# Gathering an expert's first features transposed, and reloading its first places in parts

## The chip, the cores and the metric

The kernel runs on one core of one Trainium2 chip. The metric is the device time of one execution, in microseconds (us). Before the change the median of three runs is 1217.37 us (1217.15 to 1218.14).

## What is computed

256 tokens with 2048 features pass through one layer: a gMLP mixer with its residual, then a mixture of 16 experts, two of which are chosen for each token, then an RMS norm. Of the reference, the part that matters here:

```python
def expert_block(args):
    xblk, e = args
    hid = jax.nn.silu(xblk @ w_gate[e]) * (xblk @ w_up[e])
    return hid @ w_down[e]
```

`w_gate` and `w_up` are 2048 x 1024 for each expert and `w_down` is 1024 x 2048, all float32: 25.2 MB for an expert and 403 MB for the sixteen. Each must be read once.

## The kernel before

**Mixer and router.** The mixer runs until about 290 us of the profile; its products leave the residual stream in `x` (two blocks of 128 tokens on the partitions, 2048 features along them). TensorE, ScalarE and VectorE then work out the router: scores, the two experts of each token, and the rank of each token within its expert. From the ranks VectorE builds `pick` (128 tokens by 64 slots, for each block), a selection matrix that carries the norm's scale.

**Experts as items.** An item is one expert with up to 64 of its tokens. Its weights come in twelve *units* of 2 MB (128 partitions by 4096 numbers, which are 4 rows of 1024 for gate and up): gate 0 and 1, up 0 and 1 (these four use the first half of the features, `xg_a`), gate 2 and 3, up 2 and 3 (second half, `xg_b`), then four units of `w_down`. `gate_or_up` (L1223) multiplies one unit: for each of four rows `s`, two products with 64 columns of features as the left (stationary) operand and 512 columns of weights moving. Each product in float32 is two passes in the profile. After its last product a unit increments `step_done`. So item 0 ends with step 12, and step 16 is the fourth unit of item 1.

**Features.** `gather` (L1178) multiplies `pick` (left) by `x` (moving), which gives rows of tokens in `bank[6]` and `bank[7]`; `x_row` takes a bank (ScalarE for the first half, VectorE for the second), `transpose_rows` (L1188) turns it with four transposes, and `take_half` (L879, VectorE) scales it into `xg_a` or `xg_b`. For item 0 the first half is on the way of everything that follows; for later items this is done during the item before.

**Places and loads.** There are ten places for units in `blocks` and `late` and an eleventh in `acc`. All loads are issued by SyncE on one queue, in the order written, each after a wait. The first eleven units of expert 0 fill all places. Then a load can only be issued when TensorE has used up a place: `HOMES[0]` is reloaded in three parts (row 0, row 1, rows 2 and 3; waits on `first_row_used` and on step 1), and then one unit follows on each step: expert 1's unit 1 on step 2, expert 0's last unit on step 3, expert 1's unit `n` on step `n + 2` up to unit 8, and units 9, 10 and 11 on steps 12, 13 and 14. From expert 2 on, pairs of units are loaded with one DMA of 4 MB (`load_quad`, L381), the first of them on step 16. Counted in units, 13 are loaded between the first reload and this pair.

**VectorE around it** works down a fixed program: the router's chain, `take_half(0, 0)`, then some twenty small instructions that make the table of items, a register load of the item count, `take_second_row(0)` (L933), `take_half(0, 1)`. TensorE, ScalarE and SyncE read the item count into a register as well.

Of the kernel before, what the change touches and what calls it, by code (L numbers as in the profile page):

```python
# [15 lines left out]
def hybrid_trunk_kernel(nc, x_in, norm_mix_g, norm_ffn_g, final_g, a_w_in, a_v_gain, a_w_s, a_b_s,  # L16
# [38 lines left out]
    with ExitStack() as ctx:  # L55
# [127 lines left out]
        row_loaded = [sem(f"row_loaded{s}") for s in range(2)]  # L183
        first_row_used = sem("first_row_used")
# [80 lines left out]
        FIRST_LOAD = [(single_loaded[h], 16) for h in FIRST_AT[0:SLOTS + 1]] + [(single_loaded[2], 32)]  # L265
        SECOND_AT = [SINGLES.index((unit // 2 % PAIRS, unit % 2)) for unit in range(ITEM_DOUBLES)]
        SECOND_LOAD = [(single_loaded[h], 48 if h == 2 or unit >= SLOTS else 32) for unit, h in enumerate(SECOND_AT)]
# [56 lines left out]
        def _(sp):  # L324
# [58 lines left out]
            for q in range(SLOTS + 1):  # L383
                if q == 1:

                    sp.wait_ge(mixed, HEADS)
                elif q in (3, 4, 6, 7):

                    sp.wait_ge(tile_split, KD * (PIECES - 1) + 4 * (q - 2 if q < 5 else q - 3))
                elif q == 5:  # L390

                    sp.wait_ge(tile_used, KD * (PIECES - 1) + KD // 2)
                elif q == 8:

                    sp.wait_ge(tile_used, KD * PIECES)
                elif q == 9:

                    sp.wait_ge(quarters_done, 1)
                elif q == SLOTS:

                    sp.wait_ge(sq_v_done, NB)
                load_half(0, UNIT_AT[q], HOMES[q], single_loaded[q])

            for s in range(2):

                sp.wait_ge(first_row_used, s + 1)
                sp.dma_start(HOMES[0][:, s * F:(s + 1) * F], source(1, 0)[:, s * F:(s + 1) * F]).then_inc(row_loaded[s], 16)
            sp.wait_ge(step_done, 1)
            sp.dma_start(HOMES[0][:, 2 * F:4 * F], source(1, 0)[:, 2 * F:4 * F]).then_inc(single_loaded[0], 16)

            sp.wait_ge(step_done, 2)
            load_half(1, 1, HOMES[1], single_loaded[1])
            sp.wait_ge(step_done, 3)
            load_half(0, SLOTS + 1, HOMES[2], single_loaded[2])
            for unit in range(2, SLOTS - 1):

                sp.wait_ge(step_done, unit + 2)
                load_half(1, unit, HOMES[SECOND_AT[unit]], SECOND_LOAD[unit][0])
# [94 lines left out]
        def _(act):  # L513
# [81 lines left out]
            act.wait_ge(gathered, 1)  # L595
            nc.scalar.copy(x_row, bank[6][:, :]).then_inc(row_a_ready, 1)
# [64 lines left out]
        def _(dve):  # L661
# [220 lines left out]

            count = bank[3][:, 0:E]
# [12 lines left out]
            take_half(0, 0)  # L896
# [69 lines left out]

            take_second_row(0)
# [16 lines left out]
        def _(pe):  # L984
# [189 lines left out]
            def gather(jj, halves=range(2)):  # L1174

                for b in range(NB):
                    for h in halves:
                        last = T.matmul(bank[6 + jj][h * TOK:(h + 1) * TOK, :], pick[:, b, :],  # L1178
                                        columns_of(x[:, b, jj * PIECE:(jj + 1) * PIECE], h),
                                        start=(b == 0), stop=(b == NB - 1))  # L1180
                if 1 in halves:
                    last.then_inc(gathered, 1)

            def transpose_rows(n, jj):

                pe.wait_ge((row_a_ready, row_b_ready)[jj], n + 1)
                for s in range(4):
                    last = T.transpose(bank[6 + jj][:, s * P:(s + 1) * P], every(4, x_row, s), ident[:, :])  # L1188
                last.then_inc(row_transposed, 1)
# [17 lines left out]
            gather(0)  # L1207
            gather(1, halves=(0,))
            transpose_rows(0, 0)
            gather(1, halves=(1,))  # L1210
# [3 lines left out]
            def item(i, first=False, last=False):  # L1214

                def gate_or_up(unit):
                    weights = slot_of(i, unit, last)
                    pe.wait_ge(*load_of(i, unit, last))
                    for s in range(4):
                        if isinstance(i, int) and i == 1 and unit == 0 and s < 2:  # L1220
                            pe.wait_ge(row_loaded[s], 16)
                        for c in range(2):
                            ins = T.matmul(bank[unit // 2 % 2][c * TOK:(c + 1) * TOK, :], xg(unit // 4 * 8 + unit % 2 * 4 + s),  # L1223
                                            weights[:, s * F + c * BANK:s * F + (c + 1) * BANK],
                                            start=(unit in (0, 2) and s == 0), stop=(unit in (GU - 3, GU - 1) and s == 3))
                        if first and unit == 0 and s < 2:
                            ins.then_inc(first_row_used, 1)
                    ins.then_inc(step_done, 1)

                pe.wait_ge(xg_ready, i * 2 + 1)  # L1230
                gate_or_up(0)
                if not first:
# [3 lines left out]
                for unit in range(1, 4):  # L1236
                    if not first:
                        scatter((i - 1) * 8, (2 * unit - 2, 2 * unit - 1))
                    gate_or_up(unit)
                    if first and unit == 1:  # L1240
                        transpose_rows(0, 1)
                if not first:
                    scatter((i - 1) * 8, (6, 7))
                if first:
                    pe.wait_ge(xg_ready, 2)
# [102 lines left out]
```

## Time and profile before

| what | value |
|---|---|
| median of three runs | 1217.37 us |
| the profiled execution | 1218.12 us |
| its span | 1216.1 us |
| TensorE busy | 1151.1 us, 95% of the span |
| VectorE busy | 371.8 us, 31% |
| ScalarE busy | 109.7 us, 9% |
| DMA, mean over the span | 379 GB/s, 460.70 MB |
| TensorE's granted clock | 0.990 of full speed |

The time of an execution is the span from the first to the last instruction and 2.0 us around it. The page's row of the DMA rate in 40 slices shows 150 to 360 GB/s in the mixer, 408, 330 and 367 in the three slices from 243 to 334 us, and 429 to 433 in nearly all from there to the end. A busy TensorE is no sign of a bound by itself: its passes are counted while they are in flight.

### The profile page before, as it was taken

To read this page: it belongs to the slowest core of one execution; us is meant where nothing else is said; L and a number is where in the kernel's file an instruction comes from. 1 tells how busy PE (TensorE), PEld (TensorE's weight loads), DVE (VectorE), ACT (ScalarE), POOL (GpSimd) and SP (SyncE) were. 2 spreads that over 40 slices of the span, in tenths; PEclk is the share of its full clock that TensorE was granted. 3 is DMA by queue.
4 is the path that set the end of the run, shared out by engine and by line. 5 is a ranking of instruction groups with operands and counts; after the bars stand their busy time and mean duration, and the time that the engine had idled before them with its cause. 6 is when DMAs were issued, how large, how long until landed. Compare 5 with 4: busy or idle time off the path is not lost.

```text
span 1216.1 us, 12008 instructions
## 1 busy us (share of the span) xinstructions
PE 1151.1 (95%) x5197; PEld 524.8 (43%) x5197; DVE 371.8 (31%) x560; ACT 109.7 (9%) x186; POOL 7.5 (1%) x24
## 2 busy tenths in 40 slices
PE   9999999999999999999989898989899898989986
PEld 7888877887333333333323232323232233323321
DVE  6867787776222111112111111111111111111112
ACT  1303002012010000000000000000000000000003
POOL 0200000000000000000000000000000000000000
PEclk9999999999999999999999999999999999999999
DMA  9856544598999999999999999999999999999995
GB/s 357 331 194 193 193 173 151 203 408 330 367 430 433 429 431 431 431 433 431 431 431 432 431 432 432 431 432 431 429 432 433 429 431 431 431 432 429 426 417 208
DMA packets 36303, 460.70 MB, mean 379 GB/s; under 512 B 4360, under 2 KB 5920, under 8 KB 21792
## 3 DMA queue, kind: packets, MB, share of 16 engines
q1 hardware_dynamic: 36208, 459.97, 90.9%
q8 instruction: 41, 0.67, 0.2%
q14 instruction: 6, 0.05, 0.0%
q10 hardware_dynamic: 48, 0.01, 0.0%
HBM read 457.87 MB, written 2.10 MB: 378 GB/s over the span
## 4 chain that ended last, share of the span: by engine, by line
PE 64%; DMA 32%; SPq 1%; DVE 1%; ACT 1%; issue 0%; ACTq 0%; DVEq 0%
PE bank L1223 25%; DMA blocks<-in_moe_w_gate 17%; DMA blocks<-in_moe_w_up 10%; PE bank L1286 8%; PE kept L1030 4%; PE kept L1032 4%; PE kept L1031 4%; PE bank L1030 4%; PE bank L1032 3%; PE bank L1031 3%; PE kept L1197 3%; DMA blocks<-in_moe_w_down 3%; PE kept L1178 3%; DMA late<-in_moe_w_gate 2%; PE kept L1188 1%; SPq L457 1%
## 5 line engine op out<-in xcount | busy, mean ns | idle before, releaser
L924 DVE TENSOR_TENSOR acc<-acc,kept 128x512 f32<-128x512 f32 x120 | 77.1, 684 | 455.5 <-PE kept L1197 455.5
L1223 PE MATMUL bank<-blocks,xg_a 128*64 128x512 f32 x832 | 196.4, 614 | 19.7 <-DMA blocks<-in_moe_w_gate 17.8
L1286 PE MATMUL bank<-blocks,sil 128*64 128x512 f32 x800 | 178.1, 599 | 12.2 <-DMA blocks<-in_moe_w_down 12.2
L1223 PE MATMUL bank<-blocks,xg_b 128*64 128x512 f32 x752 | 166.5, 594 | 3.2 <-DMA blocks<-in_moe_w_gate 1.6
L1223 PEld LDWEIGHTS bank<-blocks,xg_a 128*64 128x64 f32 x832 | 59.7, 140 | 149.9 <-issue 140.8
L690 DVE TENSOR_TENSOR w_lo<-blocks,w_hi 128x1024 fp32r<-128x1024 f32 x96 | 117.7, 1226 | 3.2
L1286 PEld LDWEIGHTS bank<-blocks,sil 128*64 128x64 f32 x800 | 56.1, 138 | 124.8 <-issue 104.1
L1223 PEld LDWEIGHTS bank<-blocks,xg_b 128*64 128x64 f32 x752 | 52.4, 137 | 114.6 <-issue 99.1
L951 DVE TENSOR_TENSOR sil<-sil,bank 128x512 f32<-128x512 f32 x16 | 11.0, 688 | 253.4 <-PE bank L1223 253.4
L683 DVE CAST w_hi<-blocks 128x1024 fp32r<-128x1024 f32 x96 | 67.2, 700 | 64.6 <-PE kept L1032 30.4
L1197 PE MATMUL kept<-y,back 64*128 64x512 f32 x240 | 67.7, 641 | 0.0
L1223 PE MATMUL bank<-late,xg_b 128*64 128x512 f32 x272 | 60.4, 595 | 2.8 <-DMA late<-in_moe_w_gate 2.2
L1178 PE MATMUL kept<-x,pick 128*64 128x512 f32 x256 | 62.9, 599 | 0.0
L1223 PE MATMUL bank<-late,xg_a 128*64 128x512 f32 x192 | 45.3, 614 | 5.6 <-DMA late<-in_moe_w_gate 5.4
L602 ACT ACTIVATE sil<-bank 128x512 f32<-128x512 f32 x16 | 9.6, 597 | 429.2 <-PE bank L1223 429.2
L1197 PEld LDWEIGHTS kept<-y,back 64*128 64x128 f32 x240 | 18.1, 184 | 48.9 <-issue 48.9
L1030 PE MATMUL kept<-w_hi,act_second 128*128 128x512 f32 x96 | 38.3, 398 | 0.0
L1030 PE MATMUL kept<-w_hi,act_first 128*128 128x512 f32 x96 | 38.2, 397 | 0.0
L1223 PEld LDWEIGHTS bank<-late,xg_b 128*64 128x64 f32 x272 | 18.9, 137 | 43.5 <-issue 35.7
L1030 PE MATMUL bank<-w_hi,act_second 128*128 128x512 f32 x96 | 37.6, 391 | 0.0
L1032 PE MATMUL kept<-w_hi,act_second 128*128 128x512 f32 x96 | 37.4, 390 | 0.0
L1032 PE MATMUL kept<-w_hi,act_first 128*128 128x512 f32 x96 | 37.4, 390 | 0.0
(205 smaller groups left out, 941.5 us busy)
## 6 DMA issues: line engine op xcount, KB each, us to landing
blocks<-in_moe_w_down SPq DMA_DIRECT2D x21, 4096.0 KB, 39.9
blocks<-in_moe_w_gate SPq DMA_DIRECT2D x20, 4096.0 KB, 40.1
blocks<-in_moe_w_up SPq DMA_DIRECT2D x20, 4096.0 KB, 40.2
blocks<-in_a_w_in SPq DMA_DIRECT2D x31, 1024.0 KB, 6.1
late<-in_moe_w_gate SPq DMA_DIRECT2D x6, 4096.0 KB, 34.2
late<-in_moe_w_up SPq DMA_DIRECT2D x6, 4096.0 KB, 40.6
blocks<-in_moe_w_down SPq DMA_DIRECT2D x11, 2048.0 KB, 14.6
blocks<-in_moe_w_gate SPq DMA_DIRECT2D x9, 2048.0 KB, 14.4
```

The source lines that it names most:

```text
L457: sp.dma_start(home, src).then_inc(loaded, 16)
L683: V.tensor_copy(w_hi[:, k % 2, :], raw).then_inc(hi_split, 1)
L690: V.tensor_tensor(w_lo[:, k % 2, :], raw, w_hi[:, k % 2, :].bitcast(f32), ALU.subtract)\
L924: V.tensor_tensor(acc[:, b, cols], acc[:, b, cols], bank[5 + j % 3][:, :], ALU.add)\
L1030: T.matmul(dst, hi, wh, start=(k == 0), stop=False)
L1031: T.matmul(dst, hi, wl, start=False, stop=False)
L1032: last = T.matmul(dst, lo, wh, start=False, stop=(k == KD - 1))
L1178: last = T.matmul(bank[6 + jj][h * TOK:(h + 1) * TOK, :], pick[:, b, :], columns_of(x[:, b, jj * PIECE:(jj + 1) * PIECE], h), start=(b == ...
L1188: last = T.transpose(bank[6 + jj][:, s * P:(s + 1) * P], every(4, x_row, s), ident[:, :])
L1197: T.matmul(bank[5 + j % 3][:, :], back[h * TOK:(h + 1) * TOK, b * P:(b + 1) * P], y[h * TOK:(h + 1) * TOK, jj, :], start=True, stop=True). ...
L1223: ins = T.matmul(bank[unit // 2 % 2][c * TOK:(c + 1) * TOK, :], xg(unit // 4 * 8 + unit % 2 * 4 + s), weights[:, s * F + c * BANK:s * F + ...
L1286: ins = T.matmul(bank[2 + c // 2][at:at + TOK, :], hidden, weights[:, s * D + c * BANK:s * D + (c + 1) * BANK], start=(j == 0 and s == 0), ...
```

## The change

Three things change, for item 0 and the reloads that follow it alone.

1. `gather_features` takes the place of `gather`, the copy, and `transpose_rows` for the first half of the features: `x` is the left operand (128 tokens by 128 features, every eighth) and `pick` the moving one (64 columns), so features come out on the partitions at once. It is two products for each of eight groups of features: four groups for `bank[5]` and one for `bank[6]` ahead of the first unit, three more behind it. VectorE's `take_features` scales each bank (128 by 256) into `xg_a`; the second of them stands behind the table of items. The gather of the second half (`gather(1)`) moves behind the third unit, and its transposes behind the fourth.
2. `FIRST_ORDER` exchanges the second and the third unit of expert 0: up 0 comes second, which needs the same four groups of features as gate 0.
3. The first six places are reloaded in parts (`PARTS`): places 0, 1 and 3 in rows 0, 1 and 2 to 3; places 2, 4 and 5 in two halves. The semaphore `part_used` counts the parts. It makes 15 DMAs where there were 8.

TensorE's program from the router's end to item 0's fifth unit, before (`kept` is a PSUM bank; `xg_a`, `xg_b` are the features):

```order
L1178 MATMUL kept<-x,pick 64x512 x6
L1188 MATMUL kept<-ident,y 128x128 x4
L1178 MATMUL kept<-x,pick 64x512 x2
L1212 TENSOR_LOAD before_last
L1212 ISA x2
L1223 MATMUL bank<-blocks,xg_a 64x512 x16
L1188 MATMUL kept<-ident,y 128x128 x4
L1223 MATMUL bank<-blocks,xg_a 64x512 x16
L1223 MATMUL bank<-blocks,xg_b 64x512 x16
```

And with the change:

```order
L1195 MATMUL kept<-pick,x 128x64 x10
L1237 TENSOR_LOAD before_last
L1237 ISA x2
L1247 MATMUL bank<-blocks,xg_a 64x512 x8
L1195 MATMUL kept<-pick,x 128x64 x6
L1247 MATMUL bank<-blocks,xg_a 64x512 x16
L1203 MATMUL kept<-x,pick 64x512 x4
L1247 MATMUL bank<-blocks,xg_a 64x512 x8
L1215 MATMUL kept<-ident,y 128x128 x4
L1247 MATMUL bank<-blocks,xg_b 64x512 x16
```

Eight gathering products and four transposes stood ahead of the first unit, ten small products stand there now; six small ones, four gathering ones and the transposes have moved between the units, and the transposes stand directly ahead of the fifth.

SyncE's queue behind the first eleven units, before:

```order
L407 DMA blocks<-in_moe_w_gate 128x1024 [waits first_row_used] x2
L409 DMA blocks<-in_moe_w_gate 128x2048 [waits step_done]
L373 DMA blocks<-in_moe_w_gate 128x4096 [waits step_done]
L373 DMA blocks<-in_moe_w_down 128x4096 [waits step_done]
L373 DMA blocks<-in_moe_w_up 128x4096 [waits step_done] x2
```

And with the change:

```order
L425 DMA blocks<-in_moe_w_gate 128x1024 [waits part_used] x2
L425 DMA blocks<-in_moe_w_gate 128x2048 [waits step_done]
L425 DMA blocks<-in_moe_w_gate 128x1024 [waits part_used] x2
L425 DMA blocks<-in_moe_w_gate 128x2048 [waits step_done]
L425 DMA blocks<-in_moe_w_down 128x2048 [waits part_used]
L425 DMA blocks<-in_moe_w_down 128x2048 [waits step_done]
L425 DMA blocks<-in_moe_w_up 128x1024 [waits part_used] x2
```

The same bytes go in the same order; a load that waited for its whole unit now follows row by row.

The diff, cut to its core:

```diff
         loop_half_loaded = sem("loop_half_loaded")
-        row_loaded = [sem(f"row_loaded{s}") for s in range(2)]
-        first_row_used = sem("first_row_used")
+        part_used = sem("part_used")
+        first_features_ready = sem("first_features_ready")
         ident_ready = sem("ident_ready")
...
         FIRST_HOME = [HOMES[h] for h in FIRST_AT]
-        FIRST_LOAD = [(single_loaded[h], 16) for h in FIRST_AT[0:SLOTS + 1]] + [(single_loaded[2], 32)]
+        FIRST_ORDER = [0, 2, 1] + list(range(3, ITEM_DOUBLES))
+        PARTS = {0: (1, 2, 4), 1: (1, 2, 4), 2: (2, 4), 3: (1, 2, 4), 4: (2, 4), 5: (2, 4)}
+        WHOLE = (4,)
         SECOND_AT = [SINGLES.index((unit // 2 % PAIRS, unit % 2)) for unit in range(ITEM_DOUBLES)]
-        SECOND_LOAD = [(single_loaded[h], 48 if h == 2 or unit >= SLOTS else 32) for unit, h in enumerate(SECOND_AT)]
+        RELOADS = [(1, 0), (1, 1), (0, SLOTS + 1)] + [(1, unit) for unit in range(2, SLOTS - 1)]
+
+        def reloaded(place_no):
+
+            return 16 + 16 * len(PARTS.get(place_no, WHOLE))
+
+        FIRST_LOAD = [(single_loaded[h], 16) for h in FIRST_AT[0:SLOTS + 1]] + [(single_loaded[2], reloaded(2))]
+        SECOND_LOAD = [(single_loaded[SECOND_AT[unit]], reloaded(unit if unit < 2 else unit + 1)) for unit in range(SLOTS - 1)]
+        SECOND_LOAD += [(single_loaded[SECOND_AT[SLOTS - 1 + n]], reloaded((2, 0, 1)[n]) + 16) for n in range(3)]
...
                     sp.wait_ge(sq_v_done, NB)
-                load_half(0, UNIT_AT[q], HOMES[q], single_loaded[q])
-
-            for s in range(2):
-
-                sp.wait_ge(first_row_used, s + 1)
-                sp.dma_start(HOMES[0][:, s * F:(s + 1) * F], source(1, 0)[:, s * F:(s + 1) * F]).then_inc(row_loaded[s], 16)
-            sp.wait_ge(step_done, 1)
-            sp.dma_start(HOMES[0][:, 2 * F:4 * F], source(1, 0)[:, 2 * F:4 * F]).then_inc(single_loaded[0], 16)
-
-            sp.wait_ge(step_done, 2)
-            load_half(1, 1, HOMES[1], single_loaded[1])
-            sp.wait_ge(step_done, 3)
-            load_half(0, SLOTS + 1, HOMES[2], single_loaded[2])
-            for unit in range(2, SLOTS - 1):
-
-                sp.wait_ge(step_done, unit + 2)
-                load_half(1, unit, HOMES[SECOND_AT[unit]], SECOND_LOAD[unit][0])
+                load_half(0, FIRST_ORDER[UNIT_AT[q]], HOMES[q], single_loaded[q])
+
+            parts_used = 0
+            for n, (expert, unit) in enumerate(RELOADS):
+
+                done = 0
+                for upto_row in PARTS.get(n, WHOLE):
+                    if upto_row < 4:
+                        parts_used += 1
+                        sp.wait_ge(part_used, parts_used)
+                    else:
+                        sp.wait_ge(step_done, n + 1)
+                    at = unit % 2 * 2 * HALF
+                    sp.dma_start(FIRST_HOME[n][:, done * PIECE:upto_row * PIECE],
+                                 source(expert, unit // 2)[:, at + done * PIECE:at + upto_row * PIECE])\
+                      .then_inc(single_loaded[FIRST_AT[n]], 16)
+                    done = upto_row
             for unit in range(SLOTS - 1, ITEM_DOUBLES):
...
                                      bias=red[:, b, 1:2], accum_out=red[:, b, 2:3]).then_inc(exp_done, 1)
-            act.wait_ge(gathered, 1)
-            nc.scalar.copy(x_row, bank[6][:, :]).then_inc(row_a_ready, 1)
             act.wait_ge(count_ready, 1)
...
+            def take_features(h):
+
+                V.tensor_tensor(xg_a[:, 4 * h:4 * h + 4, :], bank[5 + h][:, 0:4 * TOK].rearrange("p (s t) -> p s t", s=4),
+                                row_gain[:, 4 * h:4 * h + 4].unsqueeze(2).to_broadcast([P, 4, TOK]), ALU.mult)\
+                 .then_inc((first_features_ready, xg_ready)[h], 1)
+
...
                                  ALU.mult))
-            take_half(0, 0)
+            dve.wait_ge(gathered, 1)
+            take_features(0)
             link(V.tensor_tensor(start[:, 0, :], upto[:, 0, :], extra[:, 0, :], ALU.subtract))
...
+            dve.wait_ge(row_transposed, 1)
+            take_features(1)
             take_second_row(0)
...
-            def gather(jj, halves=range(2)):
+            def gather_features(h, rows):
+
+                for s in rows:
+                    for b in range(NB):
+                        last = T.matmul(bank[5 + h][:, s * TOK:(s + 1) * TOK], every(8, x[:, b, 0:PIECE], 4 * h + s),
+                                        pick[:, b, :], start=(b == 0), stop=(b == NB - 1))
+                return last
+
+            def gather(jj):
                 for b in range(NB):
-                    for h in halves:
+                    for h in range(2):
                         last = T.matmul(bank[6 + jj][h * TOK:(h + 1) * TOK, :], pick[:, b, :],
...
                                         start=(b == 0), stop=(b == NB - 1))
-                if 1 in halves:
-                    last.then_inc(gathered, 1)
+                last.then_inc(gathered, 1)
...
-                pe.wait_ge((row_a_ready, row_b_ready)[jj], n + 1)
+                if jj == 0:
+                    pe.wait_ge(row_a_ready, n)
+                else:
+                    pe.wait_ge(row_b_ready, n + 1)
                 for s in range(4):
...
             pe.wait_ge(pick_ready, 1)
-            gather(0)
-            gather(1, halves=(0,))
-            transpose_rows(0, 0)
-            gather(1, halves=(1,))
+            gather_features(0, range(4)).then_inc(gathered, 1)
+            gather_features(1, (0,))
             pe.wait_ge(count_ready, 1)
...
-                def gate_or_up(unit):
-                    weights = slot_of(i, unit, last)
-                    pe.wait_ge(*load_of(i, unit, last))
+                def gate_or_up(n):
+                    weights = slot_of(i, n, last)
+                    unit = FIRST_ORDER[n] if first else n
+                    pe.wait_ge(*load_of(i, n, last))
                     for s in range(4):
-                        if isinstance(i, int) and i == 1 and unit == 0 and s < 2:
-                            pe.wait_ge(row_loaded[s], 16)
                         for c in range(2):
...
                                             start=(unit in (0, 2) and s == 0), stop=(unit in (GU - 3, GU - 1) and s == 3))
-                        if first and unit == 0 and s < 2:
-                            ins.then_inc(first_row_used, 1)
+                        if first and s < 3 and s + 1 in PARTS.get(n, WHOLE):
+                            ins.then_inc(part_used, 1)
                     ins.then_inc(step_done, 1)
-                pe.wait_ge(xg_ready, i * 2 + 1)
+                if first:
+                    pe.wait_ge(first_features_ready, 1)
+                else:
+                    pe.wait_ge(xg_ready, i * 2 + 1)
                 gate_or_up(0)
-                if not first:
+                if first:
+                    gather_features(1, range(1, 4)).then_inc(row_transposed, 1)
+                else:
                     pe.wait_ge(y_ready, i)
...
                         scatter((i - 1) * 8, (2 * unit - 2, 2 * unit - 1))
+                    if first and unit == 2:
+                        pe.wait_ge(xg_ready, 1)
                     gate_or_up(unit)
-                    if first and unit == 1:
-                        transpose_rows(0, 1)
+                    if first and unit == 2:
+                        gather(1)
                 if not first:
...
                 if first:
+                    transpose_rows(0, 1)
                     pe.wait_ge(xg_ready, 2)
...
                 gate_or_up(5)

```

## Rows read from the trace of the kernel before

**Rows 1.** Stretches of the program, from the windows view; columns: engines, clock, DMA share, GB/s.

```profile
305.00:321.00 16.00, 16.00 (x76) 6.33 (x74) 6.47 (x22) 0.00 (x0) 0.00 (x0) 1.00 0.88 313
321.00:1150.00 829.00, 782.04 (x3512) 258.40 (x3509) 127.17 (x232) 50.16 (x92) 0.00 (x0) 0.99 1.00 431
```

**Rows 2.** The chain that ended last, at its end: start, us, what.

```profile
1154.90 39.13 DMA blocks<-in_moe_w_down
...
1194.08 3.65 PE bank L1298 x16
```

**Rows 3.** The same chain around expert 0 and the start of expert 1.

```profile
287.77 2.00 PE kept L1016 x16
289.77 1.91 PE bank L1151 x32
...
298.63 3.58 PE kept L1178 x12
...
302.89 1.43 PE kept L1178 x3
304.32 0.07 PE bank L1223
...
311.62 0.68 PE kept L1188 x4
312.30 13.88 PE bank L1223 x64
...
335.28 1.72 PE kept L1178 x8
...
357.65 3.58 PE bank L1223 x16
...
370.52 1.06 PE kept L1197 x4
```

**Rows 4.** The timeline of VectorE between the router and expert 0's second features.

```profile
299.98 0.19 DVE L894 TENSOR_TENSOR weight_of<-wsel,red 128x32 f32<-128x32 f32 x1
303.00 0.69 DVE L879 TENSOR_TENSOR xg_a<-kept,row_gain 128x512 f32<-128x512 f32 x1 [2.82 <-PE kept L1188]
303.61 0.17 DVE L897 TENSOR_TENSOR start<-upto,extra 128x16 f32<-128x16 f32 x1
...
309.47 0.18 DVE L917 CAST item_expert<-ids_f 128x24 int32<-128x24 f32 x1
310.69 0.69 DVE L933 COPY y<-kept 128x512 f32<-128x512 f32 x1 [1.04 <-issue]
```

**Rows 5.** Issues of loads on SyncE's queue, from its timeline.

```profile
305.64 1.19 SPq L407 DMA_DIRECT2D blocks<-in_moe_w_gate  x2
...
315.92 0.33 SPq L373 DMA_DIRECT2D blocks<-in_moe_w_down  x1
...
370.56 0.33 SPq L381 DMA_DIRECT2D blocks<-in_moe_w_gate  x1
```

**Rows 6.** Loads issued at 284.04, 287.80, 361.28, 370.56; the last column is us to landing.

```profile
blocks<-in_moe_w_up SPq DMA_DIRECT2D x1, 2048.0 KB, 7.3
...
late<-in_moe_w_down SPq DMA_DIRECT2D x1, 2048.0 KB, 9.6
...
blocks<-in_moe_w_down SPq DMA_DIRECT2D x1, 2048.0 KB, 14.3
...
blocks<-in_moe_w_gate SPq DMA_DIRECT2D x1, 4096.0 KB, 14.8
```

**Rows 7.** The DMA engines when their queue had run empty, in windows of 1 us.

```profile
283.00:284.00 1.00, 1.00 (x5) 0.56 (x3) 1.00 (x1) 0.00 (x0) 0.00 (x0) 1.00 0.00 0
284.00:285.00 1.00, 0.99 (x5) 0.80 (x5) 0.01 (x1) 0.00 (x0) 0.00 (x0) 1.00 0.23 49
285.00:286.00 1.00, 1.00 (x6) 0.81 (x5) 0.24 (x1) 0.00 (x0) 0.00 (x0) 1.00 0.89 213
```

**Rows 8.** TensorE's first wait for a load of expert weights, in the waits of 580 to 640.

```profile
PE bank L1223 <- DMA blocks<-in_moe_w_gate: 2.9, 2, 2.7
```

## The prediction, made before the changed kernel was run

> **What bounds the kernel now.** I read the windows first, then the chain that ended last, then SyncE's issues with their landings. From 321 to 1150 us the DMA engines are busy without a break and move 431 GB/s, while TensorE's clock stays at 0.99; only from 305 to 321 us do they fall to 313 GB/s [rows 1]. The chain ends in a load that lands at 1194.03, followed by expert work and the output [rows 2]. TensorE meets its first wait for a weight load between 580 and 640 us [rows 8]. So the end of the kernel is the end of a stream of loads that is full from 321 us on, and a change near 300 us is worth what it moves the *stream*, not what it moves TensorE. What the stream lost near 305 is 16 us x (1 - 313/431) = 4.4 us [rows 1]. It was lost because all places were full and the first reload waits for TensorE: the first unit starts at 304.32 [rows 3], its first rows are given back at 305.64 [rows 5]. 4.4 us is the most the change can earn there.
>
> **Term 1, the first unit starts earlier.** TensorE begins the gather at 298.63 [rows 3]. The new gather ahead of the first unit is eight products, 16 passes, each with its own load of a 128 x 128 piece of `x`. No row has just this. The nearest is L1016, also a strided 128 x 128 piece of `x` as left operand: 16 passes in 2.00 us, 0.125 us each, with 128 columns moving where here there are 64 [rows 3]. I take 0.125. From below, the router's passes cost 1.91/32 = 0.060; from above, the four scatter passes cost 1.06/4 = 0.265, and nearer, four row transposes 0.68/4 = 0.17 [rows 3]. So the bank is full at 300.6, seen by VectorE 0.1 later, at 300.7. VectorE's chain is through by then (L894 ends at 300.17 [rows 4]). `take_features` has 256 elements: between 0.19 us for 32 and 0.69 us for 512 [rows 4] that is 0.19 + 0.50 x 224/480 = 0.42. The first unit starts at about 301.2 instead of 304.32, **3.1 us earlier**. The two passes for group 4 need 0.5 us and lie beside VectorE's work. The register load on TensorE may delay this: on VectorE the whole step took 1.04 us [rows 4], from the end of L917. On TensorE it can start when `before_last` is there, some instructions before L894 (299.98 [rows 4]), and I cost it at nothing if it runs while the passes are still in the queue; without that cover, 0.3 to 0.9 us.
>
> **Term 2, what has moved between the units.** Behind the first unit stand six products, 12 passes x 0.125 = 1.5. A unit costs 3.58 behind other work and 3.43 behind a unit ((13.88 - 3.58)/3), a gather of four products 1.72, and the transposes 0.68 [rows 3]. The second bank of features costs TensorE nothing: the table of items ends 6.04 us after the first scaling's successor starts (303.61 to 309.65 [rows 4]), so at about 307.1, plus 1.04 and 0.42 is 308.6, and the third unit wants it at 301.2 + 3.43 + 1.5 + 3.58 = 309.7. If that cover goes, the third unit is late by the rest. At the fourth unit's end the second half of the features is late next: the transposes now stand directly ahead of the fifth unit, and `take_half` between them is bare: 0.11 to hand over (transposes done at 302.89 [rows 3], scaling from 303.00 [rows 4]), 0.69 [rows 4] and an estimated 0.06 back, 0.86. The fifth unit thus starts at 301.2 + 3.43 + 1.5 + 7.01 + 1.72 + 3.58 + 0.68 + 0.86 = 319.98. Before it started at 312.30 + 13.88/2 = 319.24 [rows 3]. **TensorE is 0.75 us later** from there on, although it began 3.1 us earlier: the transposed gather moves 28 passes of 0.125 (3.5 us) in the place of one gather and one turn, and the turn that was between units 2 and 3 has its scaling in the open. From the fifth unit to step 16 TensorE's chain has no wait for a load, so the 0.75 us stays.
>
> **Term 3, the reloads.** A unit's reload goes out 3.62 us after the unit starts (312.30 to 315.92 [rows 3, 5]), a row's 0.86 us per row after it. With an empty queue data flow at the full rate from about 1.4 us after the issue: 284.04, and 431 - 49 plus 431 - 213 missing in two windows [rows 7]. The stream, 4.87 us per unit of 2.1 MB, needs unit *u* issued by 305.0 + 4.87u - 1.4. The parts go out at about 302.2, 303.1 and 304.8 (u = 0, needed by 303.6), 307.2 (u = 1, by 308.5), 311.6 (u = 2, by 313.3), 315.9 (u = 3, by 318.2), 321.9 (u = 4, by 323.1). So the whole 4.4 us are won back by 321. The parts are needed for it: a whole unit at 309.8, for u = 1, would come 1.3 too late.
>
> **Term 4, the cap.** What counts is whether TensorE can keep giving back places to a stream that is 4.4 us earlier. The tight point is the first pair, 4 MB, on step 16: issued at 370.56 [rows 5], directly at the end of a unit on a chain of TensorE alone [rows 3]. It has 13 units ahead of it. Before, it landed 14.8 us after its issue [rows 6]. With an empty queue it would land after 7.3 for the first 2 MB [rows 6], and 6.1 for the second (287.80 + 9.6 less 284.04 + 7.3 [rows 6]), 13.4 together. **The slack is 1.4 us**: however early the stream is, the pair cannot land more than 1.4 us earlier than it did, plus or minus what its issue moves. By bytes alone the slack is smaller: 5.0 MB moved by 321 [rows 1], 22.2 MB more of the 13 units at 431 GB/s end at 372.6, against 370.56 + 1.4, so 0.7. With 4.87 instead of 6.1 for the second half it is 14.8 - 12.2 = 2.6. I take 1.4, as landings are what TensorE waits for, and keep 0.7 and 2.6. After the pair the issues at later steps have more room, and the DMA engines hold the kernel to its end.
>
> **Sum.** Won: 4.4 us at 321, capped at 1.4 by step 16, less the 0.75 by which step 16 is later: 0.65 us. Against the profiled execution: 1218.12 - 0.65 = 1217.5; the median shown is 0.75 below that execution, so 1217.37 - 0.65 = **1216.7 us**.
>
> By the Trainium skill (TensorE: Matmul & The Clock Gate, "LDWEIGHTS (loading the stationary operand)") a weight load takes its columns divided by 1.2 in ns, 107 ns for 128 columns, however few columns move behind it. By it 28 passes would be 0.5 us shorter than by L1016's 0.125, and the sum 1216.2; I stay with the row.
>
> **The rivals.**
> *The cap does not bind.* If step 16 comes earlier than I think, or the pair lands with the rest of the stream, what is won at 321 stays, less a gap at the reload on step 12 of some 1.4: 4.4 - 1.4 = 3.0, **1214.4**. For it: the DMA engines were busy without a gap at 372. Against it: the issue at 370.56 and its landing 14.8 later, little over the 13.4 of an empty queue.
> *TensorE's new passes are dear* (the other side). If strided loads of `x` do not hide beside so short a moving part, a pass costs the 0.265 of the scatter rows: 28 x 0.14 = 3.9 us, step 16 is 4.65 us later, less 1.4: 3.25 us slower, **1220.6**. It decides from a delay of 3.8 us, a pass of 0.235. For it: the moving part has only 64 columns to hide a load behind. Against it: L1016 loads the same kind of piece at 0.125.
> *Small parts slow the stream.* 15 loads instead of 8 for 12.6 MB. It becomes slower than before by 2.4 us if the six units lose 4.4 + 2.4 = 6.8 of their 29.2 us, below 350 GB/s. A price between 313 GB/s (with its gaps) and 431 [rows 1]: in the middle, 372, the six units lose 4.6, which takes up the 4.4 and 0.2 more, **1217.6**; at 313 they lose 11, which is the far end, 1224. Against it: parts behind others in a full queue left no dip that I can find. The Trainium skill (DMA: Bandwidth & Descriptors, "Measured (HBM→SBUF, 128 partitions, SWDGE, issued from GpSimd)") wants 1 MiB or more in a load and gives 341 GB/s for 1 MB; by it, an estimate, the six units would take 7.7 us more and the kernel 3.3 us more, 1220.7. That figure is for loads one at a time from another engine.
> *The change does not do what it says:* if the register load holds TensorE until after 301.9, step 16 moves by 1.5 and nothing is won: 1217.4.
>
> **How the numbers follow.** About 0.2% (2.4 us) is what a measurement of this kernel tells from no change, so faster means below 1214.9, slower above 1219.8. My forecast, with the register load's case in it: 0.72. Its own ends: passes at 0.060 save 0.5 ahead of the first unit (VectorE's chain holds it at 300.17) and 0.8 behind it, so step 16 is 0.5 early, and with the slack of 2.6 it is 1214.3; passes at 0.17 and the slack of 0.7 give 1217.37 + 2.0 - 0.7 = 1218.7. Cap not binding: 0.15. Dear passes: 0.07. Small parts: 0.06. The range takes most of the forecast and of the first rival: 1214.4 to 1218.7. Faster: 0.15 and 0.03 of my own tail, 0.18. Slower: 0.07 and 0.02. Same: 0.73.
>
> **What would show it.** Right: first unit at 301.2, TensorE's new passes at 0.12 to 0.13, fifth unit at 320.0, no dip of the DMA rate at 305 to 321, a new dip of some 3 to 4 us just ahead of the pair's issue at 371.3, and its landing 13.4 after that. Wrong: a rate of 431 through 366 to 373 (no cap), passes of 0.2 or more, a wait of the third unit for VectorE, or a dip that stays at 305 to 321.

## The result, and the profile after

The changed kernel takes 1222.79 us (median of five runs, 1222.40 to 1224.14), beside 1217.36 us for the kernel before in the same comparison (five runs). The ratio is 1.0052, with a 95% interval from 1.0041 to 1.0063. The change is slower, by **5.4 us** between the medians; the interval of the ratio spans 5.0 to 7.7 us. The forecast was 1216.7, with a range to 1218.7. Its profiled execution took 1224.01 us, with a span of 1221.9, against 1218.12 and 1216.1 before.

The windows view of the changed kernel, for the stretches of [rows 1] and three between them (start:end, us, then PE, PEld, DVE, ACT and POOL busy, granted clock, DMA share, GB/s):

```profile
305.00:321.00 16.00, 16.00 (x72) 7.13 (x70) 4.45 (x15) 0.00 (x0) 0.00 (x0) 0.96 0.85 275
321.00:366.00 45.00, 43.84 (x206) 15.38 (x204) 6.55 (x15) 6.70 (x8) 0.00 (x0) 1.00 1.00 410
366.00:375.00 9.00, 9.00 (x41) 2.58 (x39) 2.57 (x4) 0.00 (x0) 0.00 (x0) 1.00 1.01 431
375.00:420.00 45.00, 44.70 (x210) 15.25 (x206) 6.19 (x12) 3.11 (x6) 0.00 (x0) 1.00 0.99 418
420.00:1150.00 730.00, 683.21 (x3058) 225.26 (x3054) 112.25 (x204) 39.62 (x77) 0.00 (x0) 0.99 1.00 431
```

The stream of loads should have had no dip at 305 to 321. It has a deeper one, 275 GB/s for 313 before, and it loses again in the next 100 us; from 420 on it is the 431 GB/s of before. The bound is the same, the stream has lost more. The chain of waits says why. Its part that answers to [rows 3] (start, us, what):

```profile
298.31 4.95 PE kept L1195 x20
303.27 5.12 PE bank L1247 x16
308.39 3.00 PE kept L1195 x12
311.39 7.02 PE bank L1247 x32
318.40 1.72 PE kept L1203 x8
320.12 3.43 PE bank L1247 x16
323.56 0.69 PE kept L1215 x4
324.25 0.02 issue
324.27 0.70 DVE xg_b L887
324.97 0.04 issue
325.02 7.09 PE bank L1247 x32
```

Two things are not as forecast. The new passes (L1195) take 4.95/20 = 0.248 and 3.00/12 = 0.250 us, for 0.125. And the first unit, 16 passes that cost 3.43 to 3.58 us everywhere in [rows 3], takes 5.12. The new line by shape (duration min/median/max in ns):

```profile
L1195 PEld LDWEIGHTS kept<-pick,x x32: 312/334/336, 298.2 to 310.9; 128*128 128x128 f32 x32
L1195 PE MATMUL kept<-pick,x x32: 401/401/452, 298.2 to 311.0; 128*128 128x64 f32 x32
```

And TensorE's granted clock around the start of the first unit, in windows of the same view:

```profile
302.50:303.00 0.50, 0.50 (x4) 0.50 (x3) 0.47 (x3) 0.00 (x0) 0.00 (x0) 0.93 0.54 229
303.00:306.00 3.00, 3.00 (x9) 1.03 (x11) 2.69 (x10) 0.00 (x0) 0.00 (x0) 0.50 0.63 268
306.00:306.50 0.50, 0.50 (x4) 0.05 (x2) 0.43 (x3) 0.00 (x0) 0.00 (x0) 0.65 1.06 139
```

From about 302.9 to 306.3 it is 0.50, the lower of its two levels (1.2 for 2.4 GHz). It was 1.00 in the same windows before, and what stands ahead of the drop is TensorE busy without a gap, with the new passes. SyncE's issues answer to [rows 5]:

```profile
305.21 0.33 SPq L425 DMA_DIRECT2D blocks<-in_moe_w_gate  x1
...
376.49 0.33 SPq L391 DMA_DIRECT2D blocks<-in_moe_w_gate  x1
```

The first row of the first place goes out at 305.21 (before 305.64, forecast 302.2), the pair on step 16 at 376.49, 5.9 us later than the 370.56 before. VectorE's part was as costed: `take_features` takes 0.42 us, and the table of items ends at 308.75, long before the third unit.

### The profile page after: what moved, and what is told of

Its sections match the earlier page's. It is cut to its first block, busy times and chain, and to the rows that moved or that the text cites. A ratio compares the mean times of both kernels' runs of the same rounds, so it can differ in the third digit from the quotient of the medians.

```text
span 1221.9 us, 12056 instructions
## 1 busy us (share of the span) xinstructions
PE 1155.7 (95%) x5217; PEld 530.2 (43%) x5217; DVE 371.5 (30%) x561; ACT 109.2 (9%) x185; POOL 7.5 (1%) x24
## 4 chain that ended last, share of the span: by engine, by line
PE 62%; DMA 34%; SPq 1%; DVE 1%; ACT 1%; issue 0%; ACTq 0%; DVEq 0%
PE bank L1247 24%; DMA blocks<-in_moe_w_gate 20%; PE bank L1318 7%; DMA blocks<-in_moe_w_up 7%; DMA blocks<-in_moe_w_down 6%; PE kept L1047 4%; PE kept L1049 4%; PE kept L1048 4%; PE bank L1047 3%; PE bank L1049 3%; PE bank L1048 3%; PE kept L1224 3%; PE kept L1203 2%; DMA late<-in_moe_w_gate 2%; SPq L467 1%; PE kept L1215 1%
## 5 line engine op out<-in xcount | busy, mean ns | idle before, releaser
L1247 PE MATMUL bank<-blocks,xg_a 128*64 128x512 f32 x832 | 199.0, 622 | 20.8 <-DMA blocks<-in_moe_w_gate 19.9
L1203 PE MATMUL kept<-x,pick 128*64 128x512 f32 x248 | 59.2, 598 | 0.0
L1048 PE MATMUL bank<-w_lo,act_second 128*128 128x512 f32 x96 | 37.4, 389 | 0.0
```

Of the source, the lines that this page charges most:

```text
L1048: T.matmul(dst, hi, wl, start=False, stop=False)
```

## The experiments

The rival "TensorE's new passes are dear" had come, with something on top. **Theory A** says that the piece of `x` with every eighth feature is slow to load as a left operand, that this alone makes the pass 0.25 us and lets the clock drop, and that all that is lost follows from TensorE's delay. **Theory B** says that the short moving part (64 columns) has nothing to hide a load behind, so any such pass costs this. **Theory C** puts a share of the loss on the small reloads. Before each verdict stands what was expected; the kernel before was timed beside each (1216.77, 1217.05 and 1216.76 us in three comparisons, the first for e1 to e4, the second for e5, e7, e10 and e11, the third for the rest).

### e1: the same products, with contiguous pieces of x

```diff
-every(8, x[:, b, 0:PIECE], 4 * h + s)
+x[:, b, (4 * h + s) * P:(4 * h + s + 1) * P]
```

> The changed kernel, but the left operand of the transposed gather takes 128 consecutive features instead of every eighth; the features then stand in another order than the weights want, and nothing else differs. Theory A, the step of the left operand sets the price: a pass falls from 0.25 us to 0.12 us (12 passes behind the first unit in 1.5 us instead of 3.0), the clock stays at full speed, step 16 is issued 5 us earlier than in the changed kernel and the time is 1216.7 to 1217.5 us. Theory B, a short moving part cannot hide any load of 128 columns: 0.25 us a pass, the clock drops as before, 1222.8 us.

Measured: 1216.58 us, ratio 1.0000 [0.9991, 1.0009]. Its chain of waits, first units and fifth:

```profile
298.76 1.95 PE kept L1195 x16
...
301.28 3.65 PE bank L1247 x16
304.94 1.48 PE kept L1195 x12
...
320.04 7.09 PE bank L1247 x32
```

Its windows:

```profile
305.00:321.00 16.00, 15.22 (x78) 6.16 (x80) 4.70 (x15) 0.00 (x0) 0.00 (x0) 1.00 1.00 404
321.00:366.00 45.00, 44.63 (x210) 15.36 (x208) 6.19 (x12) 6.70 (x8) 0.00 (x0) 1.00 1.01 417
366.00:375.00 9.00, 9.00 (x40) 2.58 (x38) 2.57 (x4) 0.00 (x0) 0.00 (x0) 1.00 0.91 359
```

A pass costs 1.95/16 = 0.122 us, the clock stays at 1.00, the first unit starts at 301.28 and the fifth at 320.04. Nothing but the step between the features of the left operand was changed, so it carries the whole loss, and theory B falls: 64 columns behind a contiguous load are cheap. This is also the kernel that the forecast had described, with the dip at 305 nearly gone and a new one at 366 to 375. Its time, 1216.58 for 1216.7, flatters the forecast: beside the kernel before of its own comparison (1216.77) it won 0.2 us, not told from nothing, where 0.65 was forecast.

### e2: the reloads in parts alone, on the kernel before

```diff
-            for s in range(2):
-                sp.wait_ge(first_row_used, s + 1)
...
+            for n, (expert, unit) in enumerate(RELOADS):
+                for upto_row in PARTS.get(n, WHOLE):
...
```

> The kernel before with the reloads of the first six places in parts and nothing else of the change: TensorE's work is as before. Theory cap (the pair of loads on step 16 sets the stream): the dip at 305 to 321 shrinks by 2 to 3 us and comes back ahead of the pair's issue, gain 0.7 to 1.4 us, 1216.0 to 1216.7 us. Theory stream (what is won at 321 stays): 1214.4 to 1215. Theory small parts slow the stream: slower than 1217.4, rate under 400 GB/s at 321 to 345.

Measured: 1215.68 us, ratio 0.9995 [0.9986, 1.0004]; 360 GB/s at 305 to 321 for 313, 401 at 366 to 375 for 435. Not told from no change. The parts fill the first dip in part, and most of that is given back ahead of step 16. Theory C finds nothing here.

### e3: 26 passes more on TensorE between the fourth and the fifth unit of the kernel before

```diff
                 if first:
+                    keep_warm(4, 13)
                     pe.wait_ge(xg_ready, 2)
```

> The kernel before with 13 idle products of 128 columns (0.235 us each, 3.05 us) on TensorE between the fourth and fifth unit of expert 0, so that step 16 is 3.05 us late and the stream up to 321 us is as before. Theory cap with a slack of 0.7 to 1.4: slower by 1.6 to 2.4 us, 1219.0 to 1219.7. With a slack of 2.6: 1217.8. If step 16 does not set the stream: no change.

Measured: 1219.74 us, ratio 1.0023 [1.0012, 1.0034]. The chain shows the added wait for what it is:

```profile
319.54 3.10 PE kept L992 x26
322.64 7.02 PE bank L1223 x32
```

3.1 us of delay cost 2.8 us by the ratio and 3.0 by the medians. That is more than any of the three expectations (at most 2.4), so TensorE had nearly no slack in giving back places here. The stream runs at 412 GB/s in 321 to 366 and 406 in 366 to 375: it loses at several reloads, not at the pair alone.

### e4: every fourth feature in place of every eighth

Gate and up of expert 0 are loaded with four rows per partition, so that the left operand has a step of four. The result is the same.

```diff
-every(8, x[:, b, 0:PIECE], 4 * h + s)
+every(4, x[:, b, h * BANK:(h + 1) * BANK], s)
```

> The changed kernel with expert 0's weights for gate and up loaded with four rows of features to a partition instead of eight, so that the transposed gather takes every fourth feature (the same result is computed). Theory A, price by the step: 0.125 us a pass like the transposes with the same step, clock at full speed, step 16 at 371.3 us, 1216.7 to 1217.5 us. Theory B: 0.25 us a pass and 1222.8 us. A third, any step above one costs 0.25: as B here, while the contiguous one is cheap.

Measured: 1222.28 us, ratio 1.0039 [1.0025, 1.0052]. From its chain and its windows:

```profile
298.73 4.87 PE kept L1203 x20
303.60 5.87 PE bank L1256 x16
309.46 2.94 PE kept L1203 x12
```

```profile
302.00:303.50 1.50, 1.50 (x7) 1.41 (x7) 0.70 (x3) 0.00 (x0) 0.00 (x0) 0.50 0.89 371
303.50:308.00 4.50, 4.50 (x13) 1.40 (x14) 4.02 (x15) 0.00 (x0) 0.00 (x0) 0.50 0.78 278
```

The form of theory A that I had written down, by which a step of four loads at the transposes' price, is wrong: a pass is 0.245 us. The clock dropped earlier, inside the first gather at about 301.4, and stayed at 0.50 until about 308.2. Nearly half of the first twenty passes ran at 0.50, yet the twenty cost 4.87/20 = 0.244, and the twelve at full clock 2.94/12 = 0.245. The pass with this operand does not depend on TensorE's clock; the unit behind it does.

### e5: 128 columns moving behind the same strided pieces

```diff
-pick[:, b, :]
+pick[:, b:b + 1, :].to_broadcast([P, 2, TOK])
```

> The changed kernel with the moving operand of the transposed gather given twice, 128 columns instead of 64 (the second copy isn't read). Theory load-bound: a pass stays at 0.25 us, since the load of the strided left operand takes that long and the moving part hides beside it. If the clock fell because too little moved through TensorE in these passes, it now stays at full speed, the first unit takes 3.5 instead of 5.1 us and the time is 1.7 us below the changed kernel, about 3.7 us over the kernel before. If the moving part had been bare beside the load, a pass grows to 0.30 and the time rises by 1.5 us.

Measured: 1220.30 us, ratio 1.0027 [1.0018, 1.0037].

```profile
299.11 4.96 PE kept L1195 x20
304.06 3.58 PE bank L1247 x16
307.64 3.05 PE kept L1195 x12
```

```profile
303.00:306.00 3.00, 3.00 (x15) 1.64 (x16) 2.51 (x10) 0.00 (x0) 0.00 (x0) 1.00 0.84 360
```

Twice the columns cost nothing, so the pass waits for its load alone. And with them the clock stays at 1.00 and the first unit is back at 3.58 us. That parts the two costs: 3.25 us slower than before with the dear passes alone, 5.4 with the drop. By the chain the drop is 5.12 - 3.58 = 1.5 us in the profiled execution of the changed kernel.

### e7: the changed kernel with places 1 to 5 reloaded whole

```diff
-PARTS = {0: (1, 2, 4), 1: (1, 2, 4), 2: (2, 4), 3: (1, 2, 4), 4: (2, 4), 5: (2, 4)}
+PARTS = {0: (1, 2, 4)}
```

> The changed kernel with places 1 to 5 reloaded whole, as in the kernel before (place 0 stays in parts). Theory cap: step 16 sets the stream, so the parts are worth little here: the DMA rate at 305 to 321 falls by 40 GB/s or more and the time stays within 1 us of the changed kernel. Theory stream: it is 2 us or more slower than the changed kernel.

Measured: 1222.22 us, ratio 1.0040 [1.0026, 1.0054], against 1.0052 with the parts; the two intervals overlap. 236 GB/s at 305 to 321, but 420 at 321 to 366. The chain has the first unit longer than in the changed kernel:

```profile
303.13 5.97 PE bank L1247 x16
```

The clock was at 0.50 here from about 301.1 to 307.9, as long as in e4, so this trace holds 0.85 us of delay that has nothing to do with the parts. Neither e2 nor e7 shows a cost or a gain of the parts; the 0.6 us between the medians and this delay leave room for a share of some 1.4 us in the changed kernel. Theory C is not needed, but it isn't ruled out to the last microsecond.

### e10: contiguous pieces, features early, and the first pairs in halves

The three repairs that the runs above suggest, with the same result. Gate and up of expert 0 are loaded in the order that contiguous pieces need; the gather of the second half stands ahead of the third unit and its transposes behind it, so that VectorE's scaling lies under the fourth; and expert 2's four pairs are loaded in halves, the first of each one step earlier.

```diff
+gate_k = w_gate[0].rearrange("e (j s p) c -> p e j s c", p=P, s=4)
...
-every(8, x[:, b, 0:PIECE], 4 * h + s)
+x[:, b, (4 * h + s) * P:(4 * h + s + 1) * P]
...
                     gate_or_up(unit)
-                    if first and unit == 2:
+                    if first and unit == 1:
                         gather(1, first=True)
+                    if first and unit == 2:
+                        transpose_rows(0, 1)
...
+                if n in pair_half_loaded:
+                    for h in range(2):
+                        sp.wait_ge(step_done, 2 * (n - PAIRS + 1) + ITEM_DOUBLES - 1 + h)
+                        load_half(n // ITEM_QUADS + 1, n % ITEM_QUADS * 2 + h, QUADS[quad_at(n)][:, h, :],
...
```

> The changed kernel with three further edits: expert 0's gate and up weights are loaded in the layout in which consecutive features make a left operand (a pass of 0.12 us), the second half's gather stands ahead of the third unit and its turn behind it (its scaling no longer in the open, 0.8 us), and expert 2's first four pairs are loaded in halves, the first on the step before (the cap on step 16 moves). All the same result. If the cap is what held the stream back, 2 to 3.5 us faster than the kernel before, no dip at 366 to 375. If the cap isn't it, at most 1.2 us faster.

Measured: **1213.65 us**, ratio 0.9970 [0.9959, 0.9980], the fastest of all.

```profile
298.61 1.95 PE kept L1216 x16
...
301.13 3.65 PE bank L1271 x16
304.79 1.48 PE kept L1216 x12
306.27 3.58 PE bank L1271 x16
309.85 1.72 PE kept L1224 x8
311.57 3.43 PE bank L1271 x16
315.00 0.59 PE kept L1237 x4
315.59 10.45 PE bank L1271 x48
```

```profile
305.00:321.00 16.00, 16.00 (x82) 6.25 (x83) 4.56 (x14) 0.00 (x0) 0.00 (x0) 1.00 1.01 412
...
366.00:375.00 9.00, 9.00 (x42) 2.70 (x40) 2.57 (x4) 0.00 (x0) 0.00 (x0) 1.00 1.01 428
```

The rate shows no dip any more, and TensorE goes from the transposes into the fourth unit, and through three units, without waiting for VectorE.

### e11, e12 and e9: the halves with and without the rest

e11 is the kernel before with the parts of e2 and the halves of e10; e12 the kernel before with the halves alone; e9 is e10 without them (its expectation calls e10 the run before last).

```diff
+                if n in pair_half_loaded:
+                    for h in range(2):
...
```

> The kernel before with reloads in parts and expert 2's first four pairs in halves; TensorE's work and order as before. The parts alone won 1.3 us of DMA time by 366 and gave 0.5 back by 375. With the halves nothing is given back: 1.2 to 1.8 us faster than the kernel before. If the halves change nothing: as the parts alone, 0.5 to 1.1 us faster.

> The kernel before with expert 2's first four pairs loaded in halves, the first half one step earlier, and nothing else. In the kernel before the queue still held loads when step 16 came (no dip at 366 to 375), so by theory cap nothing is won alone: within 0.5 us of the kernel before. If issuing earlier helps by itself: 1 us or more faster.

> The kernel of the run before last but with expert 2's pairs loaded whole again, that is the changed kernel with consecutive features as left operand and the second half's gather ahead of the third unit; the same result. If step 16 caps the stream: the dip comes back at 366 to 375 (rate under 380 GB/s) and of the 3.4 us at least 1.5 are lost again, 1215 to 1216 us. If the halves were idle, 1213.7.

Measured: e11 1216.26 us, 0.9993 [0.9984, 1.0002]; e12 1217.15 us, 1.0004 [0.9995, 1.0013]; e9 1215.77 us, 0.9991 [0.9982, 1.0000]. The halves are worth nothing to a stream that comes late to step 16 (e12), and 2.1 us to one that comes early (1215.77 to 1213.65; 2.4 us if each is taken from the kernel before beside it). In e11 less came than I had expected: 0.8 us by the medians, within the interval of no change. e9 shows the cap at its clearest, since its pair is issued at the same time as before (370.49). The window around that issue:

```profile
366.00:375.00 9.00, 9.00 (x42) 2.67 (x42) 2.57 (x4) 0.00 (x0) 0.00 (x0) 1.00 0.91 359
```

### e13 and e14: what the step costs, and whom

e13 transposes the same every-eighth pieces with the identity moving (no selection, half the passes); e14 takes every second feature. One execution each.

```diff
-T.matmul(bank[5 + h][:, s * TOK:(s + 1) * TOK], every(8, x[:, b, 0:PIECE], 4 * h + s), pick[:, b, :], ...)
+T.transpose(bank[5 + h][:, s * P:(s + 1) * P], every(8, x[:, b, 0:PIECE], 4 * h + s), ident[:, :])
```

```diff
-every(8, x[:, b, 0:PIECE], 4 * h + s)
+x[:, b, 0:2 * P].rearrange("p (n s) -> p s n", s=2)[:, s % 2, :]
```

> The changed kernel, but each product of the transposed gather is a transpose by the identity of the same strided piece of x (every eighth feature, one pass each, 128 columns moving); the selection of tokens is left out. If a step of eight makes any load of the left operand slow: 0.25 us a pass. If a transpose loads its strided operand as fast as the transposes of the kernel before did with a step of four: 0.125 us, and the row I took as nearest was one of another kind.

> The changed kernel, but the left operand takes every second feature of 256 (not the features that the weights want). If the price of a product's pass grows with the step: 0.12 to 0.20 us. If any step over one has the full price, as four and eight have: 0.25 us.

Measured: 1215.45 and 1217.23 us. The line by shape, of e13 and then of e14:

```profile
L1195 PEld LDWEIGHTS kept<-ident,x x16: 185/195/207, 298.7 to 305.0; 128*128 128x128 f32 x16
```

```profile
L1195 PEld LDWEIGHTS kept<-pick,x x32: 193/196/197, 298.7 to 306.2; 128*128 128x128 f32 x32
```

A transpose loads the very piece that costs a product 334 ns in 195. The pass of a product costs 0.122 us at step 1 (e1), 0.128 at step 2 (2.05/16, e14), 0.245 at step 4 (e4), 0.248 at step 8. e14 stands for the step alone: its products use other features than the weights want. Why transposes are spared wasn't tried further and stays open.

### All runs by one measure

What the stream lost between 305 and 420 us is, summed over the four windows, their length x (1 - rate/431). For the changed kernel: 16 x (1 - 275/431) + 45 x (1 - 410/431) + 0 + 45 x (1 - 418/431) = 9.3 us.

| kernel | first unit | pair issued | stream lost | median |
|---|---|---|---|---|
| e10 | 301.13 | 365.78 (half) | 1.4 | 1213.65 |
| e9 | 301.19 | 370.49 | 3.1 | 1215.77 |
| e11 | 304.10 | 365.70 (half) | 3.2 | 1216.26 |
| e2 | 304.63 | 370.87 | 4.1 | 1215.68 |
| e1 | 301.28 | 371.52 | 4.2 | 1216.58 |
| e12 | 304.39 | 365.99 (half) | 4.3 | 1217.15 |
| before | 304.32 | 370.56 | 4.3 | 1217.36 |
| e3 | 304.55 | 374.04 | 6.3 | 1219.74 |
| e5 | 304.06 | 375.79 | 8.8 | 1220.30 |
| after | 303.27 | 376.49 | 9.3 | 1222.79 |
| e7 | 303.13 | 377.19 | 10.1 | 1222.22 |
| e4 | 303.60 | 377.51 | 10.2 | 1222.28 |

The median less what was lost lies between 1211.5 and 1213.5 us in all twelve, over a spread of 9 us (1212.3 and 1213.8 for the single executions of e13 and e14). So the time is that of a full stream and its gaps; TensorE's time matters only through them. The measure is rough, with the loss from one trace and the median from many executions: it carries differences of 5 us, and not those of 1 us.

## Why the prediction was wrong

**What bounds the kernel** was right. The table above is that reading, put to twelve kernels.

**Term 1 failed, at its first number: the pass at 0.125 us, taken from L1016.** L1016 was the wrong neighbour, although it is "also a strided 128 x 128 piece of `x`". It is a transpose, and a transpose loads a strided piece fast (e13), where a product does not. The pass measured 0.248 to 0.250. That the upper bound, the scatter's 0.265, lies so near is luck. Its rows on the page of the kernel before:

```profile
L1197 PE MATMUL kept<-y,back 64*128 64x512 f32 x240 | 67.7, 641 | 0.0
L1197 PEld LDWEIGHTS kept<-y,back 64*128 64x128 f32 x240 | 18.1, 184 | 48.9 <-issue 48.9
```

It moves 512 columns, not 64, and its load takes 184 ns, as the cheap ones do (192 in e1), not 334. No row cited in the prediction held a product that loads its left operand at a step. With passes of 0.248 the first unit could start only when all 20 passes ahead of it were through, at 303.27. Reckoned from this profile's start of the gather, 0.3 earlier than before's, the forecast was 300.9: 2.4 us late. `take_features` at 0.42 was right, and nothing shows the register load holding TensorE; e1, with cheap passes, started at 301.28 for 301.2.

**Term 2 failed by the same number**: twelve passes in 3.00 for 1.5 us. It was also incomplete: a unit priced at 3.43 took 5.12 at half clock, 1.7 more, and the clock stood in no term. The rest stands. The transposes took 0.69 for 0.68, the scaling in the open cost 325.02 - 323.56 - 0.69 = 0.77 for 0.86, and the third unit did not wait for VectorE. Together: 2.4 + 1.7 + 1.5 and 0.2 less for units and hand-overs is 5.4 us, the difference between 325.02 and the forecast 319.98 less 0.3. With the 0.75 that I had given it, and 0.3 less for the earlier router, the pair's issue was to be expected 5.8 late, and was 5.9.

By the rule of the Trainium skill (TensorE: Matmul & The Clock Gate, "LDWEIGHTS (loading the stationary operand)"), an estimate of 107 ns for a load of 128 columns, the passes would have been cheaper still. It holds roughly for e1's 0.122 us a pass, and not for a step of four or eight, with more than twice that.

**Term 3** did not get its early start, so the dip at 305 to 321 grew to 275 GB/s. With the start (e1, e9, e10) it went, to 404, 411 and 412. But not all of the 4.4 us is won even then: e1 still lacks 1.0 us at 305 to 321 and 1.5 at 321 to 366 (417 GB/s), where the term had put nothing; in e9, with the second gather earlier, it is 0.7 and 0.3. Parts in a full queue cost nothing that shows (e2, e7).

**Term 4, the cap, was right in kind** and shows in e1 and e9 where I had put it, as 9 x (1 - 359/431) = 1.5 us for the 3 to 4 forecast. Its size is not settled: I took 1.4 us of slack by the landing. In e1 the pair landed 12.1 us after an issue 1.0 later, so 1.7 us sooner than before, and the kernel won only 0.2; in e9, with its issue at 370.49, it won 1.0. So the landing of this one pair does not set the gain. What a later issue of the pair did not cost, against the kernel before beside each, is 0.5 us in e3 (0.1 by the added wait itself) and 0.5 in the change, but 1.4, 1.5 and 2.0 in e4, e7 and e5 (issued 6.95, 6.63 and 5.23 us later, slower by 5.5, 5.2 and 3.25). These runs leave the slack anywhere from 0.1 to 2.0 us, my 0.7 and my 1.4 both within.

**The rival that came** is "TensorE's new passes are dear": it decides from a pass of 0.235, and 0.248 came. Its reason, that the load does not hide beside so short a moving part, is half of it: a contiguous load behind the same 64 columns is cheap (e1), and 128 columns do not help a strided one (e5). Its price of 3.25 us is what e5 measured, whose clock did not drop; that it fits to the digit is luck, as the pass was priced from the scatter and the slack is not settled. Of the remaining 2 us of the result the drop is 1.5 to 1.7 us; what the rest is, no run shows. I gave the rival 0.07, since the row nearest by operand spoke against it, and that row was no product.

## What to carry to other kernels

Before a product with a strided left operand replaces a gather and a turn, take its price from a product that loads the same step, not from a transpose; where no row has it, lay the other operand out (here the weights, rearranged in their own load) so that the left one is contiguous. A change that frees a full stream of loads early is worth only what the next tight reload lets through, so find that reload and loosen it in the same change: the first alone gave 1.0 us here (with an interval that just reaches no change), the second alone nothing, both 3.4. And a delay of the engine that gives back places to a full queue is mostly paid: here six to nine tenths of the pair's delay came out at the end.

## What the runs showed of the hardware that I had not expected

- A product in float32 whose left operand is read at a step of 4 or 8 elements takes 0.245 to 0.250 us a pass, twice the 0.122 and 0.128 at step 1 and 2. LDWEIGHTS shows 334 ns for 192 and 196. Transposes of the same piece are spared (195 ns).
- That price does not change with the clock (0.244 over twenty passes, nearly half of them at 0.50, and 0.245 at full clock, e4), nor with 64 or 128 columns moving (e5, 4.96/20 = 0.248).
- TensorE's granted clock fell to 0.50 for 3.4 us in the changed kernel and for 6.8 in e4 and e7, though the profile shows TensorE busy without a gap over the whole gather ahead of it. It stayed at 1.00 with 128 columns moving behind the same loads (e5), and with 64 behind contiguous ones (e1). The Trainium skill (TensorE: Matmul & The Clock Gate, "Part 1: The HAM clock gate") has the clock set by how busy TensorE has been recently. These rows do not bear that out if busy is what the profile counts, since its busy share there was 1.00; why the clock fell stays open.
- A pair of 4 MB issued into an all but empty queue landed after 12.1 us (e1, e9), where the prediction had estimated 13.4.
